# Query-key products in three split passes, VectorE's orders around them, and the first four units of stage one pass by pass

## The reference

```
x = x + 0.5 * swiglu_1(rms_norm(x))                  # 2048 -> 2 x 5632 -> 2048
P = rms_norm(x) @ w_in                               # q,k,v of 8 dilated heads (A) and 8 differential heads (B)
A: q,k normed, partly rotated; s = q k^T / sqrt(128), masked by three dilated windows; softmax; @ v
B: q,k as 2 x 64; softmax(q1 k1^T) - lam * softmax(q2 k2^T); @ v
x = x + concat(rms_norm(heads)) @ w_out
x = x + 0.5 * swiglu_2(rms_norm(x))
```

## Time and profile before

| | us |
|---|---|
| median of 3 runs | 1806.03 (1805.72 to 1807.71) |
| the profiled execution's own time | 1805.4 |
| its span, first to last instruction | 1803.7 |
| TensorE busy in the span | 1797.5 (100%) |
| VectorE busy | 1551.3 (86%) |
| ScalarE busy | 1071.2 (59%) |
| DMA, mean | 195 GB/s |

### The profile page before, as it was taken

One profiled execution on the slowest core, in us unless ns is written; L12 is line 12 of the kernel. 1 busy time (PEld: TensorE's weight loads), 2 busy tenths in 40 slices (PEclk: granted clock), 3 DMA queues, 4 the chain that ended last, 5 costly groups with the idle time before them and its releaser, 6 DMA issues.

```text
span 1803.7 us, 22784 instructions
## 1 busy us (share of the span) xinstructions
PE 1797.5 (100%) x8227; PEld 1491.4 (83%) x8227; DVE 1551.3 (86%) x1614; ACT 1071.2 (59%) x1295; POOL 43.6 (2%) x73
## 2 busy tenths in 40 slices
PE   9999999999999999999999999999999999999999
PEld 7888888888888888888888888888888888888887
DVE  6899999999999888657666666799999999998986
ACT  6565665666665564556566655566666666666553
POOL 0000000000000000111010000000000000000000
PEclk9999999999999999999999999999999999999999
DMA  9665565554446566654555445755566656354654
GB/s 358 209 215 210 198 217 190 188 207 163 140 164 246 196 211 211 199 178 164 164 164 187 141 164 186 257 192 204 188 215 216 217 189 218 106 187 163 237 206 141
DMA packets 178406, 351.95 MB, mean 195 GB/s; under 512 B 7184, under 2 KB 8224, under 8 KB 178080
## 3 DMA queue, kind: packets, MB, share of 16 engines
q1 hardware_dynamic: 178304, 351.02, 55.9%
q10 hardware_dynamic: 32, 0.01, 0.0%
HBM read 348.91 MB, written 2.10 MB: 195 GB/s over the span
## 4 chain that ended last, share of the span: by engine, by line
PE 99%; DVE 0%; ACT 0%; issue 0%; POOL 0%; DVEq 0%; POOLq 0%
PE acc L537 14%; PE acc L539 14%; PE acc L538 14%; PE acc L599 8%; PE acc L598 8%; PE acc L597 8%; PE turn L611 4%; PE turn L612 4%; PE turn L610 4%; PE acc L612 3%; PE acc L611 3%; PE acc L610 3%; PE turn L568 1%; PE turn L695 1%; PE turn L694 1%; PE turn L696 1%
## 5 line engine op out<-in xcount | busy, mean ns | idle before, releaser
L1307 DVE TENSOR_TENSOR w_lo<-w_raw,w_hi 128x1024 fp32r<-128x1024 f32 x167 | 205.0, 1238 | 131.0 <-ACT w_hi L926 130.5
L926 ACT ACTIVATE w_hi<-w_raw 128x1024 fp32r<-128x1024 f32 x166 | 175.4, 1059 | 197.2 <-PE acc L539 178.2
L943 ACT ACTIVATE w_hi<-b 128x1024 fp32r<-128x1024 f32 x200 | 212.6, 1063 | 118.8 <-PE acc L599 77.2
L957 ACT ACTIVATE w_hi<-w_raw 128x1024 fp32r<-128x1024 f32 x176 | 185.5, 1059 | 121.2 <-PE acc L539 88.4
L599 PE MATMUL acc<-w_hi,h_lo 128*128 128x512 f32 x640 | 249.0, 389 | 0.0
L597 PE MATMUL acc<-w_hi,h_hi 128*128 128x512 f32 x640 | 249.0, 389 | 0.0
L598 PE MATMUL acc<-w_lo,h_hi 128*128 128x512 f32 x640 | 249.0, 389 | 0.0
L1328 DVE TENSOR_TENSOR w_lo<-w_raw,w_hi 128x1024 fp32r<-128x1024 f32 x176 | 213.0, 1222 | 31.3 <-ACT w_hi L957 27.6
L1318 DVE TENSOR_TENSOR w_lo<-b,w_hi 128x1024 fp32r<-128x1024 f32 x200 | 236.5, 1219 | 0.0
L943 ACT ACTIVATE w_hi<-w_raw 128x1024 fp32r<-128x1024 f32 x160 | 169.5, 1061 | 91.7 <-PE acc L599 64.1
L1318 DVE TENSOR_TENSOR w_lo<-w_raw,w_hi 128x1024 fp32r<-128x1024 f32 x160 | 193.8, 1222 | 15.4 <-ACT w_hi L943 12.3
(11 more groups left out here) (218 smaller groups left out, 3266.1 us busy)
## 6 DMA issues: line engine op xcount, KB each, us to landing
w_raw<-in_ffn_w_in SPq DMA_DIRECT2D x94, 1024.0 KB, 5.1
w_raw<-in_ffn_w_out SPq DMA_DIRECT2D x88, 1024.0 KB, 5.1
b<-in_ffn_w_in SPq DMA_DIRECT2D x80, 1024.0 KB, 5.1
w_raw<-in_w_in SPq DMA_DIRECT2D x48, 1024.0 KB, 5.1
w_raw<-in_w_out SPq DMA_DIRECT2D x16, 1024.0 KB, 4.9
w_raw<-in_ffn_w_in SPq DMA_DIRECT2D x4, 512.0 KB, 6.9
x_sb<-in_x SPq DMA_DIRECT2D x3, 512.0 KB, 9.0
out_y<-x_sb SPq DMA_DIRECT2D x3, 512.0 KB, 8.3
```

The lines of the kernel that those rows point to most:

```text
L926: nc.scalar.activation(w_hi[:, u % RING, 0:count, :], w_raw[:, slot, k0:k0 + count, :], ACT.Copy).then_inc(hi_ready, 1)
L943: nc.scalar.activation(w_hi[:, slot, :, :], in_raw(piece)[:, k0:k0 + UK, :], ACT.Copy).then_inc(hi_ready, 1)
L957: nc.scalar.activation(w_hi[:, u % RING, :, :], src, ACT.Copy).then_inc(hi_ready, 1)
L1307: nc.vector.tensor_tensor(w_lo[:, slot, 0:count, :], w_raw[:, v // 2 % RAW, k0:k0 + count, :], w_hi[:, slot, 0:count, :].bitcast(F32), ALU ...
```

## The change

- `scores` no longer multiplies float32: the rounded queries and keys `qk_hi` (ScalarE, `round_qk`) and their rest `qk_lo` (VectorE, the new `split_qk`) go through three passes, and the order of the loops is t, pass, c instead of c, t. `scores` and `values` wait for `qk_split`.
- `norm_heads` becomes `head_factors` (the dependent operations) and `scale_heads` (the products). For the first two groups the factors stay where they were and the products go one step later; for the third both go to phase 0 of head 13.
- `scale_qk` goes from the end of iterations 6 and 9 to their beginning, ahead of `turn_mixed`.
- ScalarE's copy of the last values chunk goes behind `round_qk(12)` and `copy_w_t(11)`.
- Units 0 to 3 of the first stage go pass by pass (`early_unit`), each pass after its own wait; `norm_in` is turned before the first block of `x`, and the second part of that block is turned inside the first unit.

```diff
+            def early_pass(v, w, lhs, kks, start=False):
+                for kk in kks:
+                    k = UK * v + kk
+                    for t in range(TT):
+                        mm = nc.tensor.matmul(acc[0][:, t, :], lhs[:, k, t * P:(t + 1) * P], w[:, v, kk, :],
+                                              start=start and kk == 0, stop=False)
+                return mm
+            def early_unit(v, split, count):
+                pe.wait_ge(hi_ready, v + 1)
+                early_pass(v, w_hi, h_hi, range(UK))
+                pe.wait_ge(split, count)
+                early_pass(v, w_hi, h_lo, range(UK))
+                pe.wait_ge(lo_ready, v + 1)
+                early_pass(v, w_lo, h_hi, range(UK)).then_inc(units_used, 1)
             def first_unit():
+                pe.wait_ge(half_hi, 1)
+                pe.wait_ge(first_hi, 1)
+                early_pass(0, w_hi, h_hi, range(1), True)
+                pe.wait_ge(x_landed[0], 16)
+                turn_x(0, xg_at[0], range(2, 4)).then_inc(rows_turned, 1)
+                pe.wait_ge(hi_ready, 1)
+                early_pass(0, w_hi, h_hi, range(1, UK))
                 pe.wait_ge(half_split, 1)
...
+                early_pass(0, w_hi, h_lo, range(UK))
+                pe.wait_ge(first_split, 1)
+                early_pass(0, w_lo, h_hi, range(1))
+                pe.wait_ge(lo_ready, 1)
+                early_pass(0, w_lo, h_hi, range(1, UK)).then_inc(units_used, 1)
...
-                    pe.wait_ge(turn_split, 1)
-                    chunk(PARTS_D, u0, range(1, 2), h, 0)
-                    pe.wait_ge(c1_half_split, 1)
-                    chunk(PARTS_D, u0, range(2, 3), h, 0)
+                    pe.wait_ge(turn_hi, 1)
+                    early_unit(1, turn_split, 1)
+                    pe.wait_ge(c1_half_hi, 1)
+                    early_unit(2, c1_half_split, 1)
                     turn_norm(2, 1)
-                    pe.wait_ge(turn_split, 2)
-                    chunk(PARTS_D, u0, range(3, 4), h, 0)
+                    pe.wait_ge(turn_hi, 2)
+                    early_unit(3, turn_split, 2)
...
             def scores(u):
-                pe.wait_ge(qk_t_ready, u + 1)
+                pe.wait_ge(qk_split, u + 1)
...
-                for c in range(subs):
-                    part = slice(c * width, (c + 1) * width)
-                    for t in range(TT):
-                        mm = nc.tensor.matmul(score[:, c, t, :], qk_t[part, 0, t * P:(t + 1) * P],
-                                              qk_t[part, 1, :], start=True, stop=True)
+                for t in range(TT):
+                    for n, (q, k) in enumerate(((qk_hi, qk_hi), (qk_hi, qk_lo), (qk_lo, qk_hi))):
+                        for c in range(subs):
+                            part = slice(c * width, (c + 1) * width)
+                            mm = nc.tensor.matmul(score[:, c, t, :], q[part, 0, t * P:(t + 1) * P], k[part, 1, :],
+                                                  start=n == 0, stop=n == 2)
...
             def values(u):
-                    pe.wait_ge(qk_t_ready, u + 2)
+                    pe.wait_ge(qk_split, u + 2)
...
             warm(12)
+            pe.wait_ge(norm_landed, 16)
+            nc.tensor.transpose(turn[0][:, 0:KD], norm_in[:, :], ident[0:KD, 0:KD]).then_inc(norm_turned, 1)
             pe.wait_ge(x_half_landed, 16)
             turn_x(0, xg_at[0], range(2)).then_inc(half_turned, 1)
-            pe.wait_ge(norm_landed, 16)
-            nc.tensor.transpose(turn[0][:, 0:KD], norm_in[:, :], ident[0:KD, 0:KD]).then_inc(norm_turned, 1)
             warm(10)
-            pe.wait_ge(x_landed[0], 16)
-            turn_x(0, xg_at[0], range(2, 4)).then_inc(rows_turned, 1)
...
-            copy_chunk(3 * GROUPS - 1)
             for s, n, count in tail():
                 attention_step(s - 1)
+                if s == SEG * (GROUPS - 1) + 1:
+                    copy_chunk(3 * GROUPS - 1)
                 split_hi(PROJ, n + 4, n + count + 4, PARTS_D)
...
+            def split_qk(u):
+                dve.wait_ge(qk_hi_ready, u + 1)
+                if u == 0:
+                    dve.wait_ge(col_ready, 3)
+                for a in range(2):
+                    n = a + (TT if u < B_HEADS else 0)
+                    s = nc.vector.scalar_tensor_tensor(qk_lo[:, a, :], qk_turn[:, a, :], gain_col[:, n:n + 1],
+                                                       qk_hi[:, a, :].bitcast(F32), ALU.mult, ALU.subtract)
+                s.then_inc(qk_split, 1)
...
             def attention_step(s):
                 u, phase = divmod(s, 3)
+                if phase == 0 and u < HEADS:
+                    split_qk(u)
...
-                if phase == 2 and 0 < u < HEADS and u % HEADS_C == 0:
-                    norm_heads(u // HEADS_C - 1)
+                g = u // HEADS_C - 1
+                if phase == 2 and 0 <= g < GROUPS - 2 and u % HEADS_C == 0:
+                    head_factors(g)
+                if phase == 0 and 0 <= g < GROUPS - 1 and u % HEADS_C == 1:
+                    if g == GROUPS - 2:
+                        head_factors(g)
+                    scale_heads(g)
...
                     if s >= 0:
                         attention_step(s)
+                    if j in (6, 9):
+                        scale_qk(2 * g + j // 9)
                     if turned_at(s):
                         turn_mixed(s)
...
-                    if j in (6, 9):
-                        scale_qk(2 * g + j // 9)
```

More of the change, by code:

```diff
@@ L226, in hybrid_layer_kernel @@
             weights = sb("weights", [P, TT, SEQ], F32, attention)
-            qk_t = sb("qk_t", [P, 2, SEQ], F32, attention)
+            qk_hi = sb("qk_hi", [P, 2, SEQ], F32R, attention)
             w_t = sb("w_t", [P, TT, SEQ], F32, attention)
@@ L244, in hybrid_layer_kernel @@
             norm_in = sb("norm_in", [KD, P], F32, attention)
+            qk_lo = sb("qk_lo", [P, 2, SEQ], F32R, attention)
         acc = [ctx.enter_context(nc.psum_tensor(f"acc{i}", [P, TT, NC], F32)) for i in range(2)]
@@ L323, in hybrid_layer_kernel @@
         qk_turned = sem("qk_turned")
-        qk_t_ready = sem("qk_t_ready")
+        qk_hi_ready = sem("qk_hi_ready")
+        qk_split = sem("qk_split")
         scored = sem("scored")
@@ L622, in sum_of @@
                 return s_hi[:, n - 1], s_lo[:, n - 1]
-            def first_unit():
-                pe.wait_ge(half_split, 1)
[L627 to L631, removed]
-                    for t in range(TT):
[L633 to L638, removed]
+            def early_pass(v, w, lhs, kks, start=False):
[12 more added lines that the diff above has]
+                early_pass(v, w_lo, h_hi, range(UK)).then_inc(units_used, 1)
+            def first_unit():
+                pe.wait_ge(half_hi, 1)
[5 more added lines that the diff above has]
+                early_pass(0, w_hi, h_hi, range(1, UK))
+                pe.wait_ge(half_split, 1)
+                early_pass(0, w_hi, h_lo, range(UK))
[3 more added lines that the diff above has]
+                early_pass(0, w_lo, h_hi, range(1, UK)).then_inc(units_used, 1)
             def hidden_first(s_in, r0):
@@ L1158, in copy_chunk, with round_qk @@
                     nc.scalar.activation(squares[:, :, :], qkv[:, g % 2, kind, :, :], ACT.Square).then_inc(qk_squared, 1)
-            def copy_qk_t(u):
+            def round_qk(u):
                 act.wait_ge(qk_turned, u + 1)
@@ L1167, in copy_qk_t @@
                     n = a + (TT if u < B_HEADS else 0)
-                    s = nc.scalar.activation(qk_t[:, a, :], qk_turn[:, a, :], ACT.Copy, scale=gain_col[:, n:n + 1])
-                s.then_inc(qk_t_ready, 1)
+                    s = nc.scalar.activation(qk_hi[:, a, :], qk_turn[:, a, :], ACT.Copy, scale=gain_col[:, n:n + 1])
+                s.then_inc(qk_hi_ready, 1)
             def exps(u):
@@ L1216, in attention_step @@
                     if u < HEADS:
-                        copy_qk_t(u)
+                        round_qk(u)
                     if 1 <= u <= HEADS:
@@ L1769, in finish_weights, with head_factors, scale_heads @@
                 s.then_inc(weights_ready, 1)
-            def norm_heads(g, first=0, last=HEADS_C):
+            def head_factors(g, first=0, last=HEADS_C):
                 dve.wait_ge(head_copied, HEADS_C * g + last)
                 inverse_root(head_rstd[:, TT * first:TT * last], head_ss[:, TT * first:TT * last], HD)
+            def scale_heads(g, first=0, last=HEADS_C):
                 for n in range(first, last):
@@ L1796, in attention_late @@
                     if u == HEADS - 1:
-                        norm_heads(GROUPS - 1, 0, HEADS_C - 1)
+                        head_factors(GROUPS - 1, 0, HEADS_C - 1)
+                        scale_heads(GROUPS - 1, 0, HEADS_C - 1)
                     if u == HEADS:
-                        norm_heads(GROUPS - 1, HEADS_C - 1)
-                if phase == 2 and 0 < u < HEADS and u % HEADS_C == 0:
-                    norm_heads(u // HEADS_C - 1)
```

(4 more changed lines are left out.)

## The result

| | before | changed |
|---|---|---|
| median, us (6 runs each) | 1806.95 (1805.72 to 1807.71) | 1814.89 (1813.28 to 1816.18) |
| profiled execution, its span | 1805.4, 1803.7 | 1813.49, 1811.8 |
| mean granted clock | 1.000 | 0.998 |

The changed kernel is slower: ratio 1.0045, interval 1.0035 to 1.0056. Forecast were 1809.8 and 1805.8 to 1813.0: the sign was right, the time lies above the range. Of the 4.2 us between the forecast's sum (1809.3) and the profiled execution, the clock alone makes 3.3.

A forecast was written before the change was run, and what follows sets the result against it. TensorE, busy 1797.5 of 1803.7 us, was taken as the bound. 1805.4 - 1.2 (start) - 2.3 (scores) + 3.5 + 2.5 (turns) + 1.4 (tail) = 1809.3, given as 1809.8 us for the median, range 1805.8 to 1813.0.

The forecast's parts named there:

- The waits at the turns: Turns of mixed rows, groups 2 and 3: TensorE waits for turn_mixed behind scale_qk, +3.5 and +2.5 us.
- The tail's wait: Tail: TensorE's turn of group 2's rows waits for ScalarE's copy, held up by later factors and products, +1.4 us.
- The scores: Scores of 16 heads: six rounded passes or pairs at 0.120 us replace four float32 steps of 0.216, -2.3 us.
- pairs for B: Kind B scores, eight heads over 64-row groups: passes run side by side, six pairs a head instead of twelve single passes.
- a pass of A: Kind A scores, eight heads, six single passes each: 0.120 us forecast; by the skill's rule 0.107 + 0.109, +3.4 us.
- Rival 1: Turns: VectorE is through before TensorE asks, so no wait there; 1802.5 us, chance 0.08.
- rival 3: Scores: 64-row passes don't pair (1815.7 us) or a short pass is no shorter (1820.2 us); chance 0.09.
- The first product and the next transposes: Start: first product forecast near 7.0 us instead of 8.20, next transposes at 10.3 instead of 11.05.
- the start: First units: earlier first product gives 0.7 us and unit 2's vanished wait 0.5, together -1.2 us.
- rival 2: Turn of group 2: the clock falls after the 3.5 us wait, costing 2.0 us; 1811.8 us, chance 0.12.
- four units of lead: At j = 9: splits pushed back by scale_qk have 10.9 us of lead, so the delay costs nothing.
- Rival 4: Start: it gives nothing because later units wait for VectorE instead; 1811.1 us, chance 0.08.

The follow-up runs named there:

- the order put back: Changed kernel with scale_qk following turn_mixed again at j = 6 and 9: 1804.89 us, 0.6 below before, ratio 0.9999.
- the filled waits: Changed kernel with 26 and 16 idle transposes inside TensorE's waits at the turns of groups 2 and 3: 1809.94 us, ratio 1.0027.
- The kernel with early rests: Kernel with turn_mixed in front and early tail factors, plus split_qk before the second split_lo at j = 6 and 9: 1801.31 us, ratio 0.9977.
- the scores alone: Kernel before with only three-pass scores and split_qk, old orders of VectorE and ScalarE: 1825.07 us, 19.6 above before, ratio 1.0105.

## Why the prediction was wrong

**The steps that held.** The waits at the turns: 3.5 and 2.5 forecast, 3.35 and 2.36 measured once the clock's part is taken away; the difference is the 0.2 us for the signal, which is 0.05. The mechanism, `scale_qk`'s 4.88 us in front of `turn_mixed`, is shown by the order put back. The tail's wait, +1.4 forecast, +1.6 measured. The scores: 0.120 a pass and pairs for B, -2.7 us against -2.3. By the Trainium skill's rule that a weight load overlaps running products only in another row group (TensorE: Matmul & The Clock Gate, The mechanism) a pass of A would have cost 0.216 (the prediction's estimate); it steps by 0.12, so the trace disagrees. Rival 1 (no wait) and rival 3 (no pairs) are out. The first product and the next transposes came within 0.05 us of their times, and the start gained 1.5 instead of 1.2. Being this near is in part luck, as the start's gain varies by 1.1 us between traces.

**The step that failed is rival 2 ("The clock falls in the longest wait"), its chance and its place.** It had a chance of 0.12, and "by it this rival comes true at group 2, and only there". The sum put the clock at nothing, and it fell at both turns: 1.7 + 1.6 us by the filled waits. Without these 3.3 us the median would be 1811.6, inside the range. I had argued from a mean clock of 1.000 "with the waits that it has", of which none after POOL's first 1.4 us is longer than 0.7, and from 3.5 us being less than the 3.95 that the clock took to rise. Neither bears on it. The first says nothing of longer waits, and this view of the clock doesn't even show the slow start (it gives 1.00 for 0 to 5.5 us, where transposes step by 0.21). The second compares falling with rising. The Trainium skill (TensorE: Matmul & The Clock Gate, Why this matters for your kernels) warns of gaps between bursts. The trace agrees at 3.17 us, and goes further: the clock fell behind 2.15 us too, a shorter gap than those that the page warns of. The clock belonged into the price of each wait, 1.7 us at even chances at least.

**Two covers that weren't there.** That "the splits that `scale_qk` pushes back have four units of lead (10.9 us): nothing" is true of `w_lo`, but `split_qk` stands behind them, and `values` waits for it: +1.2 us at heads 2, 3 and 7. For `split_qk` the prediction took the copy of a chunk as the longest work ahead of it, not `scale_qk` with two `w_lo` behind:

```profile
839.21 0.86 DVE L1761 SCALAR_TENSOR_TENSOR qk_lo<-turn,gain_col,qk_hi 128x256 fp32r<-128x256 f32 x2
```

```profile
840.22 1.13 PE L853 MATMUL turn<-qkv,w_t 128*128 128x128 f32 x8 [0.38 <-DVE qk_lo L1761]
```

The kernel with early rests shows it: this loss is gone there. And of the start, 0.5 came back at a load. Rival 4 had named VectorE for this; it was a DMA, and a third of the gain.

**The sum again**, by measured terms: -1.0 start, -2.7 scores, +1.2 rests late, +5.7 turns' waits, +3.3 clock, +1.6 tail = +8.1.

Against the forecast's sum of +3.9: +3.3 clock, +1.2 rests, +0.5 load, -0.3 start, -0.4 scores, -0.3 turns' waits, +0.2 tail, together +4.2. The median lies another 1.4 above the profiled execution, where I had allowed 0.6.

Not settled: what decides between fall and no fall behind waits of 1.9 us, and why this median lies so far above its profiled execution; the loads of the start, which vary, are one candidate.

## What to carry to other kernels

Where TensorE is the bound, a new wait costs its length and, from about 2 us as here, perhaps a stretch at half clock behind it (1.7 us); what can't be removed can be filled with idle transposes. When an operation is moved ahead on a full engine, ask not only for its old neighbours but for the new short operation that now stands behind it. Here a norm (a reduction, twelve small operations and two products, 4.88 us together) in front of one operation of 1.2 us cost 9.0 us, more than the kernel lost in all. And with several waits made by one reordering, take them away one at a time: the same change with three operations of VectorE placed otherwise is 4.3 us faster than before instead of 7.9 slower.

## What the runs showed of the hardware

- The clock fell to 1.2 GHz behind waits of 3.17 and 2.15 us and behind three of six waits of 1.90 to 2.00 us and one of 2.67 (the scores alone); behind waits of 0.3 to 1.74 us it never fell in these traces. It stayed low for 3.4 us each time. In the changed kernel the falls came 0.1 and 0.7 us after TensorE had begun again.
- With TensorE kept busy by transposes for half of the same waits, it didn't fall in any of eight runs.
- Passes over 64 rows in different halves of the array overlap even when they are issued three places apart, and a lone one takes as long as one over 128 rows (0.115 us for 256 columns).
- A late start behind 512-column products costs 0.24 us more than the idle time in front of it (four places, idle 0.02 to 0.39 us).
